# Two transformer blocks on one core: tile homes of short cross layers, a rounded softplus sum, and splits and copies moved

## The reference

```
def stick_breaking_branch(q, k, v):            # branch b of the merge, 8 heads
    z = q k^T * scale ; strict = s < t
    log_not = where(strict, log_sigmoid(-z), 0)         # = -softplus(z)
    later = reversed cumsum(log_not) - log_not
    a = where(strict, exp(log_sigmoid(z) + later), 0) ; out = a v
dsa_branch:   # branch a: latent attention over the 64 best keys of an index score
short_conv_branch: B * causal_depthwise_conv3(C * h)    # branch c
merged = sum_i sigmoid(g_i) * (y_i @ w_branch_i) ; out = merged @ w_out
```

## Time and profile before

| | us |
|---|---|
| median of 3 runs | 2249.3 (2249.2 to 2253.29) |
| the profiled execution | 2250.69 |
| its span, first to last instruction | 2248.9 |
| TensorE busy | 2215.1 (98%) |
| VectorE busy | 1436.8 (64%) |
| ScalarE busy | 1065.0 (47%) |

### The profile page before, as it was taken

The page is one execution under the profiler, slowest core; times in us unless marked ns, Lnnn a source line. Parts: engine busy times, 40 slices in busy tenths (PEclk is TensorE's granted clock), DMA queues, the critical chain, the costliest instruction groups (busy, mean ns, idle before and its releaser), DMA issues.

```text
span 2248.9 us, 38296 instructions
## 1 busy us (share of the span) xinstructions
PE 2215.1 (98%) x16065; PEld 2055.7 (91%) x16065; DVE 1436.8 (64%) x1679; ACT 1065.0 (47%) x1290; POOL 105.4 (5%) x174
## 2 busy tenths in 40 slices
PE   9999999999999999999999999999999999999998
PEld 9979899888989989998998998999998998998997
DVE  6875656577665555556866676556556865676555
ACT  4554444356444443443555454443443556454442
POOL 2300000000000000000011000000000002000000
PEclk9999999999999999999999999999999999999999
DMA  7656555663655665566452755565665543664553
GB/s 245 213 178 206 166 177 193 195 182 131 195 172 161 199 228 171 188 218 199 153 172 88 237 188 179 188 216 178 196 204 192 182 151 116 202 229 150 188 178 122
DMA packets 348523, 411.90 MB, mean 183 GB/s; under 512 B 11452, under 2 KB 280952, under 8 KB 348224
## 3 DMA queue, kind: packets, MB, share of 16 engines
q1 hardware_dynamic: 339184, 377.19, 52.0%
q0 software_dynamic: 9168, 32.26, 4.4%
HBM read 406.51 MB, written 5.00 MB: 183 GB/s over the span
## 4 chain that ended last, share of the span: by engine, by line
PE 90%; DVE 5%; issue 2%; ACT 2%; DMA 1%; DVEq 0%; ACTq 0%; SPq 0%
PE bank L355 90%; ACT wh L1244 1%; DVE wl L1772 1%; DVE x L1886 0%; DVE z L1881 0%; DVE stat L1847 0%; DVE front_l L1772 0%; DVE z L1845 0%; PE bank L1210 0%; ACT prob L1722 0%; DMA raw<-in_w_branch 0%; DMA raw<-in_w_mix_in 0%; DVE nmax L2416 0%; DVE en_l L1772 0%; DVE em_l L1772 0%
## 5 line engine op out<-in xcount | busy, mean ns | idle before, releaser
L1772 DVE TENSOR_TENSOR wl<-raw,wh 128x2048 fp32r<-128x2048 f32 (+1 forms) x352 | 762.8, 2172 | 515.9 <-ACT wh L1244 434.3
L355 PE MATMUL bank<-xl,wh 128*128 128x256 f32 x3144 | 878.9, 280 | 3.8 <-DVE logit L2388 1.3
L355 PE MATMUL bank<-xh,wh 128*128 128x256 f32 x3144 | 870.5, 277 | 0.0
L355 PE MATMUL bank<-xh,wl 128*128 128x256 f32 x3144 | 870.5, 277 | 0.0
L1244 ACT ACTIVATE wh<-raw 128x2048 fp32r<-128x2048 f32 (+1 forms) x352 | 637.9, 1817 | 318.9 <-PE bank L355 293.7
L355 PEld LDWEIGHTS bank<-xl,wh 128*128 128x128 f32 x3144 | 590.4, 188 | 10.9 <-issue 6.7
L355 PEld LDWEIGHTS bank<-xh,wl 128*128 128x128 f32 x3144 | 590.0, 188 | 2.0 <-issue 1.4
L355 PEld LDWEIGHTS bank<-xh,wh 128*128 128x128 f32 x3144 | 590.4, 188 | 0.2
L355 PE MATMUL bank<-wl,hh 128*128 128x512 f32 x528 | 205.9, 390 | 0.0
L355 PE MATMUL bank<-wh,hh 128*128 128x512 f32 x528 | 205.5, 389 | 0.0
L355 PE MATMUL bank<-wh,hl 128*128 128x512 f32 x528 | 205.4, 389 | 0.0
(11 more groups left out here) (387 smaller groups left out, 3136.2 us busy)
## 6 DMA issues: line engine op xcount, KB each, us to landing
raw<-in_ffn_w_in SPq DMA_DIRECT2D x80, 1024.0 KB, 5.2
raw<-in_w_mix_in SPq DMA_DIRECT2D x56, 1024.0 KB, 5.4
raw<-in_ffn_w_gu SPq DMA_DIRECT2D x40, 1024.0 KB, 5.2
raw<-in_ffn_w_out SPq DMA_DIRECT2D x40, 1024.0 KB, 5.1
raw<-in_ffn_w_down SPq DMA_DIRECT2D x20, 1024.0 KB, 5.1
raw<-in_mem_wkv SPq DMA_DIRECT2D x16, 1024.0 KB, 5.5
raw<-in_even_w_in SPq DMA_DIRECT2D x13, 1024.0 KB, 6.8
raw<-in_w_branch SPq DMA_DIRECT2D x24, 512.0 KB, 3.4
```

The source lines that it names most:

```text
L355: ins = pe.transpose(o, a, b) if transpose else pe.matmul(o, a, b, start=start, stop=stop)
L1772: dve.tensor_tensor(part_of(t, 1), raw_tile(t), part_of(t, 0).bitcast(F32), ALU.subtract)\
```

## The change

Nothing in what is computed changes, except that the softplus is summed as two rounded parts, high and low.

1. Later-sums: `ones_r` and `tge_r` are rounded copies, `sp_h` and `sp_l0`/`sp_l1` the parts of softplus; ScalarE makes the high part, VectorE the low one; TensorE makes six products per head.
2. Convolution taps: a function of their own, called behind the subtractions of pairs 1 and 3.
3. ql copies in front of the exponentials of the same step.
4. Even mixer: look 3 behind unit 3 on VectorE.
5. Long cross layers: before the second residual of block 0 VectorE splits entry tiles up to 1, the third after x of block 0.
6. Short cross layers: entry tile 0 goes to "note", tile 1 to "mem"; "note" is free from the layer's start. Tile 0 is split before the T copies (ScalarE) and the head outputs (VectorE), tile 1 behind the head outputs. ScalarE takes the copies of xv. The look-ahead behind the queries is 3. The transposes of x block 0 come when 2 blocks are left.

```diff
-                    if todo == BESIDE and enters:
+                    if todo == (BESIDE if kc > 4 else 2) and enters:
...
-            return (["front", "side", "back"][:n], []) if SUB[j][0] == "ffn" else (["mem", "note"], ["front"])
+            if SUB[j][0] == "ffn":
+                return ["front", "side", "back"][:n], []
+            return ["note", "mem"] if SUB[j][:2] == ("cross", 2) else ["mem", "note"], ["front"]
...
@@ TensorE, single_cross @@
+            free_after["note"] = len(ring)
...
-            for slot in ("mem", "note"):
-                free_after[slot] = len(ring)
+            free_after["mem"] = len(ring)
...
@@ TensorE, merge @@
+            pe.wait_ge(sig("sums_rounded"), l_ + 1)
-                    pe.wait_ge(sig("softplus_masked"), 8 * l_ + u + 1)
+                    pe.wait_ge(sig("softplus_low"), 8 * l_ + u + 1)
-                    mm(o[:, 0:S], tge[:, :], sp[:, 0:S], True, False)
-                    mm(o[:, P:S], ones[:, :], sp[:, S:W3], False, True)
-                    mm(o[:, S:W3], tge[:, :], sp[:, S:W3], True, True, ("later", l_, u))
+                    mm(o[:, 0:S], tge_r[:, :], sph[:, 0:S], True, False)
+                    mm(o[:, 0:S], tge_r[:, :], spl[:, 0:S], False, False)
+                    mm(o[:, P:S], ones_r[:, :], sph[:, S:W3], False, False)
+                    mm(o[:, P:S], ones_r[:, :], spl[:, S:W3], False, True)
+                    mm(o[:, S:W3], tge_r[:, :], sph[:, S:W3], True, False)
+                    mm(o[:, S:W3], tge_r[:, :], spl[:, S:W3], False, True, ("later", l_, u))
...
@@ ScalarE, single_cross @@
+            ahead(("xq", j, 1), PARTS)
             for u in range(4):
                 g = unit[0] + u
...
+            def value_copy(t):
+                name = ("xv", j, t, 0)
+                o = get(name, None)
+                free(name, act.activation(xv[:, t, 0:512], o[:, :], ACT.Copy))
+
+            value_copy(0)
+            split_to(entry_tiles[j + 1][0])
             for u in range(4):
                 name = ("T", unit[0] + u)
...
+                if u == 0:
+                    value_copy(1)
             for u in range(4):
                 name = ("O", unit[0] + u)
...
-            split_to(entry_tiles[j + 1][0])
+            split_to(entry_tiles[j + 1][1])
...
@@ ScalarE, merge @@
+            def softplus_high(pair):
+                for u in (2 * pair, 2 * pair + 1):
+                    wait("softplus_masked", 8 * l_ + u + 1)
+                    act.activation(sp_h[:, u % 2, :], prob[:, u % 2, 0:W3], ACT.Copy)\
+                       .then_inc(sig("softplus_high"), 1)
             heads("qa", 0)
+            wait("merge_loaded", 32 * (l_ + 1))
+            act.activation(ones_r[:, :], ones[:, :], ACT.Copy)
+            act.activation(tge_r[:, :], tge[:, :], ACT.Copy).then_inc(sig("sums_rounded"), 1)
...
             heads("qs", 1)
+            softplus_high(0)
...
                 filler(l_, 2 * pair)
+                if pair < 3:
+                    softplus_high(pair + 1)
                 filler(l_, 2 * pair + 1)
...
@@ VectorE, out_proj @@
-                    split_to(entry_tiles[j + 1][0 if single and t == 0 else -1])
+                    split_to(entry_tiles[j + 1][1 if SUB[j][0] == "cross" and t == 0 else -1])
-                if single and t == 0:
-                    split_to(entry_tiles[j + 1][1])
+                if SUB[j][:2] == ("cross", 1) and t == 0:
+                    split_to(entry_tiles[j + 1][-1])
...
@@ VectorE, softmax @@
-                    ahead(("S", unit[0] + min(t, n_units - 1)))
+                    ahead(("S", unit[0] + min(t, n_units - 1)), PARTS if t == 3 else PARTS - 1)
...
@@ VectorE, single_cross @@
-            for t in range(TB):
-                name = ("xv", j, t, 0)
-                o = get(name, None)
-                free(name, dve.tensor_copy(xv[:, t, 0:512], o[:, :]))
+            ahead(("xq", j, 1), PARTS)
+            split_to(entry_tiles[j + 1][0])
             for u in range(4):
                 name = ("O", unit[0] + u)
...
-            split_to(entry_tiles[j + 1][0])
+            split_to(entry_tiles[j + 1][1])
...
@@ VectorE, merge @@
+            def softplus_low(pair):
+                for u in (2 * pair, 2 * pair + 1):
+                    wait("softplus_high", 8 * l_ + u + 1)
+                    dve.tensor_tensor((sp_l0, sp_l1)[u % 2][:, :], prob[:, u % 2, 0:W3],
+                                      sp_h[:, u % 2, :].bitcast(F32), ALU.subtract)\
+                       .then_inc(sig("softplus_low"), 1)
             softplus(0)
+            softplus_low(0)
...
+                if pair % 2:
+                    conv_taps(l_, pair // 2)
                 filler(l_, 2 * pair)
+                if pair < 3:
+                    softplus_low(pair + 1)
                 filler(l_, 2 * pair + 1)
```

More of the change, by code:

```diff
@@ L224, in program @@
     cks = sb("cks", [P, 4], F32, st)
+    ones_r = sb("ones_r", [P, P], F32R, st)
+    st.close()
+    st = ExitStack()
+    sb("gap_sx", [P, 3 * W3], F32, st)
+    sp_l1 = sb("sp_l1", [P, W3], F32R, st)
+    sb("gap_sy", [P, P + 4 * S], F32, st)
+    sp_h = sb("sp_h", [P, 2, W3], F32R, st)
+    sp_l0 = sb("sp_l0", [P, W3], F32R, st)
+    tge_r = sb("tge_r", [P, P], F32R, st)
     st.close()
@@ L1121, in merge @@
             await_read(("vs", l_, 0), ("vs", l_, 1))
+            pe.wait_ge(sig("sums_rounded"), l_ + 1)
             for pair in range(4):
                 for u in (2 * pair, 2 * pair + 1):
-                    pe.wait_ge(sig("softplus_masked"), 8 * l_ + u + 1)
+                    pe.wait_ge(sig("softplus_low"), 8 * l_ + u + 1)
                     o = take(("later", l_, u))
-                    sp = prob[:, u % 2, :]
-                    mm(o[:, 0:S], tge[:, :], sp[:, 0:S], True, False)
-                    mm(o[:, P:S], ones[:, :], sp[:, S:W3], False, True)
-                    mm(o[:, S:W3], tge[:, :], sp[:, S:W3], True, True, ("later", l_, u))
+                    sph, spl = sp_h[:, u % 2, :], (sp_l0, sp_l1)[u % 2][:, :]
+                    mm(o[:, 0:S], tge_r[:, :], sph[:, 0:S], True, False)
[4 more added lines that the diff above has]
+                    mm(o[:, S:W3], tge_r[:, :], spl[:, S:W3], False, True, ("later", l_, u))
                 if pair < 3:
@@ L1716, in merge @@
                     free(("T", g), act.activation(probT[:, g % 2, 0:W3], o[:, 0:W3], ACT.Copy))
+                if t % 2 and t < 7:
+                    for u in (t + 1, t + 2):
+                        o = get(("ql", l_, u))
+                        free(("ql", l_, u), act.activation(ql[:, u % 2, :], o[:, 0:S], ACT.Copy))
                 if 0 <= t < 8:
@@ L1724, in merge @@
                     ins.then_inc(sig("exp_done"), 1)
[L1725 to L1728, removed]
                 if t >= 4 and t % 2:
@@ L2276, in odd, with conv_taps @@
             out_proj(j)
+        def conv_taps(l_, n):
+            y = two(bm[:, 1, :])
+            await_read(("ch", l_, n))
+            for tap in range(3):
+                for k in range(2):
+                    r = ROWS["conv_w_2"] + l_ * 12 + tap * 4 + 2 * n + k
+                    w = pc[:, r:r + 1]
+                    if tap == 0:
+                        ins = dve.tensor_scalar(y[:, k, :], zc[:, k, 0:S], w, None, ALU.mult)
+                    else:
+                        ins = dve.scalar_tensor_tensor(y[:, k, :], zc[:, k, tap:tap + S], w, y[:, k, :],
+                                                       ALU.mult, ALU.add)
+                link(ins)
         def conv_tile(l_, i):
@@ L2289, in conv_tile @@
                 free(name, dve.tensor_tensor(zc[:, :, 2:2 + S], y, two(o[:, :]), ALU.mult))
[L2290 to L2300, removed]
             else:
```

## The result

| | before | after |
|---|---|---|
| median, us | 2249.25 (2248.83 to 2253.29, 4 runs) | 2235.56 (2233.01 to 2237.7, 4 runs) |
| ratio, 95% interval | | 0.9932 [0.9921, 0.9944] |
| profiled execution, us | 2250.69 | 2237.7 |
| span, us | 2248.9 | 2235.9 |

The account below looks back on a forecast made before the run. TensorE was taken as the bound, busy 2215.1 of 2248.9 us. Terms -3.1 - 1.6 + 0.2 - 2.7 - 2.1 + 0.8 - 3.8 - 3.7 = -16.0 took 2249.3 to 2233.3 us, range 2228 to 2242.

Parts of the forecast that it names:

- Later-sums: Merges: six rounded products a head at 0.11 us each replace three float32 products, -3.1 us over eight pairs.
- Rivals 2 and 5: Later-sums: narrow rounded products cost like float32, 6.8 us worse, chance 0.08; or by their columns, 3.5 us better, chance 0.07.
- The 0.1 us a merge for pair 2: Merges, pair 2: charge for the filler's bank coming late behind ScalarE's added copies, 0.2 us for both merges.
- Taps, ql, even mixer: Taps behind the subtractions, -1.6 us; ql copies before the exponentials, -2.7; even mixer's weight split done earlier, -2.1.
- Long cross layers: Exits of two long layers: waits before block 0's transposes vanish, but the gain is given back at block 1, +0.8 us.
- Short cross layers and the clock: Two short exits: x of block 1 comes 1.9 us earlier, -3.8 us; the clock no longer falls behind it, -3.7 us.
- Rival 1: Behind the short exits the clock still falls: all but the last term, -3.7 us, holds, 2237.0 us; chance 0.12.
- move along and stay: Branch section: stalls of about 1.3 us at 1248 and 1937 hang on a moved chain and remain.
- Rivals 3 and 4: Short layers give back 7.5 us, chance 0.12; softplus low part stalls TensorE in merge pairs, 24.6 us, chance 0.04.

Follow-up runs that it names:

- b1_wl_late: The kernel after with one VectorE weight split per merge moved behind the subtractions of pair 2: ratio 0.9935, median 2233.81 us.
- parts 2 to 4: The kernel before with only taps moved, ql copies first and the even mixer's look-ahead 3: ratio 0.9963, -8.3 us.
- a5_even: The kernel before with only look-ahead 3 behind unit 3 in the even mixer: ratio 0.9989, -2.5 us.
- b2_long_fill: The kernel after with the third entry tile's split in the long cross layers moved before the low halves of block 0: ratio 0.9927, median 2231.71 us.
- a3_long: The kernel before with only the long cross layers' third entry tile split behind x of block 0: ratio 1.0009, +2.0 us.
- b3_short_fill: The kernel after with the short cross layers' third entry tile split between the low halves of block 0: ratio 0.9934, median 2233.29 us.
- the first four experiments: The kernel before with later-sums alone, short cross layers alone, long cross layers alone, or taps, ql and even mixer alone: ratios 0.9995, 0.997, 1.0009, 0.9963.

## Why the prediction was right, and where it was off

The direction and the range held, and the forecast, at 0.57 the likeliest case, came. Its sum was 2.3 us too large by the medians, 3.0 by the spans and 0.7 by the ratio. By the spans the 3.0 are 1.6 of pair 2, 1.1 of the branch section and 1.1 of the spacing of products, less small terms that came out better. Part of the closeness is luck: in this profile no exit lost its clock.

- **Later-sums**: predicted -3.1, measured -3.4 in the eight pairs. 0.11 us for each narrow product, taken from the 200-column rows, was right as a mean, and the exchange of products shows that it is the right way to count. The pair of the earlier trace rows at 1.85 stood for all, but pairs 1 and 2 took 1.95 before, 1.51 after. Rivals 2 and 5 are out. The 81 ns that the Trainium skill ("TensorE: Matmul & The Clock Gate", Back-to-back issue gap) gives for 128 columns is not seen here: single narrow products start their successor after 57 to 114 ns (203 in front of z), and the six of a head take 113 ns each in the mean.
- **The 0.1 us a merge for pair 2** is the term that was mis-sized: it measured 0.88. The walk had seen the chain (sp_h, then the high half, then wl, then the subtraction) and counted on VectorE's 1.3 to 1.8 us of lead. But VectorE was idle in front of this wl for ScalarE's half in the earlier trace rows already, 1.17 us, and is so after, 1.06: here ScalarE sets the time, and it has 0.9 us of copies more. In the two traces VectorE's product for y (bm) comes 3.7 us earlier (1138.35, 1134.63), wl and the subtraction only 2.9 (1144.19, 1141.30), and TensorE asks 4.2 us earlier. b1_wl_late shows that nothing else held TensorE there. Cost: 1.6 us, about half of the 3.0 between the spans.
- **Taps, ql, even mixer**: -1.6, -2.7 and -2.1 predicted; -1.6, -2.7 and -2.3 in the trace, each wait gone and nothing late next. Not foreseen: the wait of the even mixer pulled the clock down in 2 of 4 profiles, at 1.6 us each; that may be part of why parts 2 to 4 gave 8.3 us by the runs, but a5_even, -2.5 us, is too coarse to show it.
- **Long cross layers**: +0.8 predicted, +0.7 in both traces that have the part, by the mechanism given: the waits moved from block 0 to block 1, at 1.14 and 0.62 us. VectorE was the bound, and b2_long_fill, which only fills its idle 1.39 us, turned the loss into a gain.
- **Short cross layers and the clock**: -3.8 and -3.7 predicted, -3.8 and -3.7 in this pair of profiles. The exits were walked rightly (1.26 us of wait for "about 1.4" with its hidden part, xv 0.21 for 0.3). "With the stall cut to about 1.4 us I expect no fall" was too firm: it falls in 4 of 12 such exits instead of 10 of 10, at 1.6 us each in the mean. That makes -2.1 us for the two exits in the mean (an estimate from these counts), so 1.6 of the -3.7 was luck of the two profiles: before had one of the two longest falls, after had none. Rival 1, at 0.12, comes true in one exit of two in some executions. The argument against it also misread its row: the pairs of waits in the long layers before are 0.60 and 0.79 us, not over 1 us like those it was to speak for.
- **Branch section**: that its waits "move along and stay" held in the experiments (1.0 to 1.3 us idle); in the profile of the kernel after one of them was 2.11. This is the landing time of its tile, 6.2 us in this profile and 5.1 to 5.3 in the twelve others; the kernels don't differ in it, and why one took longer stays open.
- Rivals 3 and 4: in no profile did a low part of the softplus, or a split pulled forward at the short exits, hold TensorE.

## What to carry to other kernels

When a chain of two engines is moved earlier, walk both: the lead of the one is worth only as much as the other's part of the chain comes earlier too. Where one engine set the pace of an exit, moving work along its list gave nothing (a3_long), but moving it into that engine's idle time did, even where it made a smaller wait elsewhere (b2_long_fill, b3_short_fill). Price the clock behind a wait of TensorE by how often it falls, from several profiles, not by one.

## What the hardware showed beyond that

- The same wait sometimes lowers the granted clock and sometimes not: 1.95 us in 2 of 4, 1.26 and 0.62 us in 4 of 12, and a fall to the lower level (1.2 of 2.4 GHz) costs 1.0 to 2.4 us, mostly 1.5 to 1.6. The Trainium skill ("TensorE: Matmul & The Clock Gate", What's actually happening) says of the start of a kernel that the same one shows 6, 11 or 14 slow products from run to run; the traces show such a spread behind a wait: of two profiles of the kernel after, one has a fall at a short exit and one has none. Of the kernel before, on the chip of the first four experiments, the runs with mean clock 0.995 took 2252.2 to 2254.6 us and those with 0.998 took 2249.0 and 2249.4; on another chip runs with 0.998 took 2250.7 and 2252.0, so the clock is not the whole of it.
- Rounded products of 256 columns lie 113 or 118 ns apart at granted clock 1.00, in long stretches of one or the other: of the 9432 products of xh or xl with tiles of the ring about 1580 stand at the longer step before, 1820 after, 1620 in the second profile of the same kernel, 1100 in b2_long_fill. At 5 ns each that is 1.0 us between two executions of one kernel and up to 3.6 us between executions of different ones. What sets the step was not found.
